# First chunk of two column tiles summed on TensorE, their loads issued sooner, and matmuls on constants ahead of and between the first column sums

## The reference

```python
mod = c @ w_mod + b_mod
shift, scale, gate = jnp.split(mod, 3, axis=-1)
u = x * (1.0 + scale[:, None, :]) + shift[:, None, :]
proj = u @ w_in
q, k, v, z_a, cb, cc, cx, z_b, g_a, g_b = jnp.split(proj, SEG_SPLITS, axis=-1)
...
h = sigmoid(g_a) * (yA @ P_a) + sigmoid(g_b) * (yB @ P_b)
out = h @ w_out
y = LayerNorm(alpha * x + gate[:, None, :] * out)
```

## Time and profile before

| | |
|---|---|
| median of 3 runs | 1502.29 us (1502.23 to 1502.61) |
| the profiled execution | 1502.2 us, of which the span of instructions is 1500.5 us |
| TensorE busy | 1477.4 us, 98% of the span |
| VectorE, ScalarE, GpSimd busy | 864.6, 511.9, 48.5 us |
| HBM read and written | 211.33 and 7.34 MB |

### The profile page before, as it was taken

The page is one execution under the profiler, slowest core; times in us unless marked ns, Lnnn a source line. Parts: engine busy times, 40 slices in busy tenths (PEclk is TensorE's granted clock), DMA queues, the critical chain, the costliest instruction groups (busy, mean ns, idle before and its releaser), DMA issues.

```text
span 1500.5 us, 18355 instructions
## 1 busy us (share of the span) xinstructions
PE 1477.4 (98%) x6592; PEld 1210.0 (81%) x6592; DVE 864.6 (58%) x1190; ACT 511.9 (34%) x724; POOL 48.5 (3%) x91
## 2 busy tenths in 40 slices
PE   6999999999999999999999999999999999999996
PEld 5888888878888788887888878888788888888885
DVE  7987877567565675656746568333432323444447
ACT  2334654253442534425344253232122221421120
POOL 0000000000000000000000000100000000000000
PEclk9999999999999999999999999999999999999999
DMA  9999543443544425444254442542223232363222
GB/s 355 392 330 318 189 117 116 137 136 90 161 120 136 137 86 154 130 133 140 84 152 134 133 141 78 188 150 91 84 88 108 92 103 85 110 252 112 84 84 112
DMA packets 211974, 219.18 MB, mean 146 GB/s; under 512 B 8417, under 2 KB 160353, under 8 KB 211169
## 3 DMA queue, kind: packets, MB, share of 16 engines
q1 hardware_dynamic: 200736, 176.72, 36.1%
q0 software_dynamic: 10096, 35.66, 7.8%
q10 hardware_dynamic: 1106, 6.32, 1.0%
HBM read 211.33 MB, written 7.34 MB: 146 GB/s over the span
## 4 chain that ended last, share of the span: by engine, by line
PE 97%; DVE 1%; SPq 1%; DMA 1%; issue 0%; ACT 0%; DVEq 0%
PE acc L1336 30%; PE acc L1338 30%; PE acc L1337 30%; PE sc L1468 1%; PE misc L1491 1%; PE sc L1336 1%; PE sc L1338 1%; PE sc L1337 1%; PE sc L1482 1%; DMA raw<-in_w_in 1%; SPq L388 0%; DVE mod_sum L840 0%; PE misc L1474 0%; PE misc L1338 0%; PE misc L1336 0%; PE misc L1337 0%
## 5 line engine op out<-in xcount | busy, mean ns | idle before, releaser
L1336 PE MATMUL acc<-act_hi,w_hi 128*128 128x512 f32 x1472 | 577.9, 393 | 2.7 <-DVE act_lo L887 2.7
L1338 PE MATMUL acc<-act_hi,w_lo 128*128 128x512 f32 x1472 | 573.8, 390 | 0.0
L1337 PE MATMUL acc<-act_lo,w_hi 128*128 128x512 f32 x1472 | 573.7, 390 | 0.0
L524 ACT ACTIVATE w_hi<-raw 128x1024 fp32r<-128x1024 f32 (+2 forms) x258 | 268.2, 1047 | 745.1 <-PE acc L1338 572.7
L813 DVE TENSOR_TENSOR w_lo<-raw,w_hi 128x1024 fp32r<-128x1024 f32 x254 | 306.5, 1215 | 370.0 <-ACT w_hi L524 369.5
L1336 PEld LDWEIGHTS acc<-act_hi,w_hi 128*128 128x128 f32 x1472 | 276.9, 188 | 64.4 <-DVE w_lo L813 4.4
L1338 PEld LDWEIGHTS acc<-act_hi,w_lo 128*128 128x128 f32 x1472 | 276.7, 188 | 58.2
L1337 PEld LDWEIGHTS acc<-act_lo,w_hi 128*128 128x128 f32 x1472 | 276.9, 188 | 56.9 <-issue 0.2
L1069 DVE SCALAR_TENSOR_TENSOR bias_acc<-bias_w,mod,bias_acc 128x512 f32<-128x512 f32 x48 | 36.0, 751 | 124.5 <-DMA bias_w<-in_w_in 124.5
L1336 PE MATMUL acc<-y_hi,w_hi 128*128 128x512 f32 x256 | 99.7, 389 | 0.0
L1338 PE MATMUL acc<-y_hi,w_lo 128*128 128x512 f32 x256 | 99.6, 389 | 0.0
(11 more groups left out here) (182 smaller groups left out, 1090.4 us busy)
## 6 DMA issues: line engine op xcount, KB each, us to landing
raw<-in_w_in SPq DMA_DIRECT2D x258, 256.0 KB, 6.3
raw<-in_w_tail SPq DMA_DIRECT2D x32, 1024.0 KB
raw<-in_w_in SPq DMA_DIRECT2D x25, 1024.0 KB
w_mod_in<-in_w_mod SPq DMA_DIRECT2D x32, 512.0 KB, 8.7
w_mod_in<-in_w_mod SPq DMA_DIRECT2D x16, 1024.0 KB, 7.7
gate_in<-in_w_mod POOLq DMA_DIRECT2D x32, 512.0 KB, 4.1
bias_w<-in_w_in POOLq DMA_DIRECT2D x48, 256.0 KB, 3.3
res<-in_x ACTq DMA_DIRECT2D x1, 4096.0 KB, 14.8
```

The lines of the kernel that those rows point to most:

```text
L524: return act.activation(dst, src, ACT.Copy)
L1336: pe.matmul(dst, a_hi, b_hi, start=first, stop=False)
L1337: pe.matmul(dst, a_hi, b_lo, start=False, stop=False)
L1338: return pe.matmul(dst, a_lo, b_hi, start=False, stop=last)
```

## The change

- **TensorE at work on constants.** VectorE sets `cos`, 512 columns wide, to 1/128 as its first instruction (before: 128 columns, later). When that is done, TensorE runs 4 float32 matmuls on it with 256 moving columns (`keep_awake(4)`), and one more after each of the first three chunks of `first_columns`. They write to `acc`, which the first products overwrite.
- **Chunk 4 (chunk 0 of group 1) summed by TensorE.** After `first_products(0, 0)`, `direct_columns` sums it for k tiles 2 and 3, by 8 float32 matmuls of moving size 1 into two columns of `misc`. VectorE leaves its four steps out, and adds the two columns to the bias just before it sums the last chunk of group 1 (`add_direct_sums`).
- **Loads.** Chunk 4 is issued between the first tiles 0 and 1; chunks 8 to 11 go ahead of x and the raw weights of group 2. The two raw pieces of tile 0 have a semaphore each.
- **VectorE's order.** `pair_columns(1)` stands ahead of `lo_half(2)`, and all four chunks of group 2 ahead of `lo_half(4)` and `lo_half(5)`.
- **TensorE's order.** For group 2 the first of the three `sc` tiles of `gate_half(1)` is done ahead of `reduce_sums(2)`, the other two behind it.

```diff
-            for n in range(MOD_CHUNKS):
+            scale_chunk(MOD_CHUNKS)
+            first_tile(1)
+            for n in range(1, MOD_CHUNKS):
                 scale_chunk(MOD_CHUNKS + n)
             x_pair(1)
             pair_unit(1)
-            for g in range(2, GROUPS):
+            for n in range(MOD_CHUNKS):
+                scale_chunk(2 * MOD_CHUNKS + n)
+            x_pair(2)
+            pair_unit(2)
+            for g in range(3, GROUPS):
...
+            dve.memset(cos[:, :], 1.0 / P).then_inc(means_set, 1)
             own(dve.memset(eps_col[:, :], EPS))
...
+            def add_direct_sums():
+
+                dve.wait_ge(b_ready, 1)
+                dve.wait_ge(direct_sums, 1)
+                own(dve.tensor_tensor(b_col[:, KT + 2:KT + 4], misc[:, 2 * KT:2 * KT + 2], b_col[:, KT + 2:KT + 4],
+                                      ALU.add))
+                settle()
...
-            for n in range(MOD_CHUNKS):
+            for n in range(DIRECT, MOD_CHUNKS):
+                if n == MOD_CHUNKS - 1:
+                    add_direct_sums()
                 scale_sums(1, n)
+            pair_columns(1)
             lo_half(2, 0, 0, 0)
-            pair_columns(1)
             scaled_lo(1)
             lo_half(3, 0, 0, 0)
-            scale_sums(2, 0)
-            scale_sums(2, 1)
-            scale_sums(2, 2)
+            for n in range(MOD_CHUNKS):
+                scale_sums(2, n)
             lo_half(4, 0, 0, 0)
             lo_half(5, 0, 0, 0)
-            scale_sums(2, 3)
...
+            def keep_awake(times):
+
+                for _ in range(times):
+                    pe.matmul(acc[:, 0, 0:2 * P], cos[:, 0:P], cos[:, 0:2 * P], start=True, stop=True)
+
+            pe.wait_ge(means_set, 1)
+            keep_awake(4)
             pe.wait_ge(ones_set, 1)
...
                     ins.then_inc(first_sums, 1)
+                    if n < MOD_CHUNKS - 1:
+                        keep_awake(1)
...
+            def direct_columns():
+
+                pe.wait_ge(mod_ready, 2)
+                for k in range(2):
+                    for n in range(DIRECT):
+                        pe.wait_ge(scale_landed[MOD_CHUNKS + n], 16)
+                        for a in range(MOD_STEPS):
+                            e = MOD_STEPS * n + a
+                            ins = pe.matmul(misc[:, 2 * KT + k:2 * KT + k + 1],
+                                            scale_in(MOD_CHUNKS + n)[:, a, k * P:(k + 1) * P], c_col[:, e:e + 1],
+                                            start=(e == 0), stop=(e == DIRECT * MOD_STEPS - 1))
+                ins.then_inc(direct_sums, 1)
+
             first_columns()
             first_products(0, 0, acc_banks)
+            direct_columns()
             first_products(0, 1, sc_banks)
             first_products(1, 0, acc_banks)
             for g in range(1, GROUPS):
+                if g == 2:
+                    gate_half(1, (0,))
                 reduce_sums(g, 2, misc[:, 2 * g:2 * g + 2])
                 if g == 1:
                     first_products(1, 1, sc_banks)
                 else:
-                    gate_half(g - 1)
+                    gate_half(g - 1, (1, 2) if g == 2 else range(G_TILES))
```

More of the change, by code:

```diff
@@ L60 @@
 SHIFTS = D // COLS
-SCALE_STEPS = GROUPS * MOD_CHUNKS * MOD_STEPS
+DIRECT = 1
+SCALE_STEPS = (GROUPS * MOD_CHUNKS - DIRECT) * MOD_STEPS
 Y_PARTS = (((0, 1024), (1024, 2048)),) * (NT - 1) + (((0, 1024), (1024, 1664), (1664, 2048)),)
@@ L231, in decoder_block @@
         first_x = sem("first_x")
-        first_raw = sem("first_raw")
+        first_raw = [sem(f"first_raw{n}") for n in range(2)]
         first_hi = sem("first_hi")
@@ L235, in decoder_block @@
         first_sums = sem("first_sums")
+        direct_sums = sem("direct_sums")
+        means_set = sem("means_set")
         b_ready = sem("b_ready")
@@ L375, in first_tile @@
                 row = w_in[k * P:(k + 1) * P, GATE_A:GATE_A + (4 + G_TILES) * P]
-                landed, each = (raw_landed[0], 32) if k else (first_raw, 16)
-                sp.dma_start(raw[:, 0, k, :], row[:, 0:COLS]).then_inc(landed, each)
-                sp.dma_start(raw[:, 0, 2 + k, 0:G_TILES * P], row[:, COLS:COLS + G_TILES * P]).then_inc(landed, each)
+                for n, (c0, c1) in enumerate(((0, COLS), (COLS, (4 + G_TILES) * P))):
+                    sp.dma_start(raw[:, 0, 2 * n + k, 0:c1 - c0], row[:, c0:c1]
+                                 ).then_inc(raw_landed[0] if k else first_raw[n], 32 if k else 16)
             def scale_chunk(c):
                 g, n = divmod(c, MOD_CHUNKS)
[L383 to L386, removed]
+                before = c - SCALE_SLOTS
+                if 0 <= before < MOD_CHUNKS:
+                    sp.wait_ge(first_sums, before + 1)
+                    sp.wait_ge(mod_step, MOD_STEPS * (before + 1))
+                elif MOD_CHUNKS <= before < MOD_CHUNKS + DIRECT:
+                    sp.wait_ge(direct_sums, 1)
+                elif before >= MOD_CHUNKS + DIRECT:
+                    sp.wait_ge(mod_step, MOD_STEPS * (before + 1 - DIRECT))
                 rows = w_mod[n * MOD_STEPS * P:(n + 1) * MOD_STEPS * P, D + g * G_COLS:D + (g + 1) * G_COLS]
@@ L582, in _ @@
                     else:
-                        act.wait_ge(first_raw, 32)
+                        act.wait_ge(first_raw[f], 16)
                     copy(w_hi[:, f, k, 0:width], raw[:, 0, 2 * f + k, 0:width]).then_inc(hi_ready if k else first_hi, 1)
@@ L826, in _, with steps_before, sum_chunk @@
             dve.wait_ge(c_in, 16)
-            def sum_chunk(q, n, rows, width, sums):
+            def steps_before(q):
+                return MOD_STEPS * (MOD_CHUNKS * q - (DIRECT if q > 1 else 0))
+            def sum_chunk(q, n, rows, width, sums, first=0):
                 for a in range(MOD_STEPS):
-                    e = MOD_STEPS * (MOD_CHUNKS * q + n) + a
+                    e = steps_before(q) + MOD_STEPS * (n - first) + a
                     dst = mod_sum[:, q % 2, a % sums, 0:width]
                     scale = c_col[:, MOD_STEPS * n + a:MOD_STEPS * n + a + 1]
-                    if n == 0 and a < sums:
+                    if n == first and a < sums:
                         if q >= 2:
@@ L850, in scale_sums @@
                 dve.wait_ge(scale_landed[c % SCALE_SLOTS], 16 * (c // SCALE_SLOTS + 1))
-                sum_chunk(g, n, scale_in(c), G_COLS, 2)
+                sum_chunk(g, n, scale_in(c), G_COLS, 2, DIRECT if g == 1 else 0)
                 if n == MOD_CHUNKS - 1:
-                    dve.wait_ge(mod_step, MOD_STEPS * MOD_CHUNKS * (g + 1))
+                    dve.wait_ge(mod_step, steps_before(g + 1))
                     both = mod_sum[:, g % 2, 0, 0:G_COLS], mod_sum[:, g % 2, 1, 0:G_COLS]
@@ L862, in shift_sums @@
                 if n == MOD_CHUNKS - 1:
-                    dve.wait_ge(mod_step, MOD_STEPS * MOD_CHUNKS * (GROUPS + j + 1))
+                    dve.wait_ge(mod_step, steps_before(GROUPS + j + 1))
                     dve.sem_inc(sums_ready, 1)
@@ L947, in bring_down @@
                 dve.tensor_scalar(table[:, :], table[:, :], -3.1415925, None, ALU.max).then_inc(trig_ready, 1)
-            own(dve.memset(cos[:, 0:P], 1.0 / P))
-            settle()
+            dve.wait_ge(means_set, 1)
             own(dve.tensor_copy(mean_mat[:, :], cos[:, 0:P]))
@@ L1361, in half, with gate_half @@
                         ins.then_inc(bank_full[n], 1)
-            def gate_half(g):
+            def gate_half(g, tiles=range(G_TILES)):
                 f = 2 * g + 1
                 pe.wait_ge(lo_ready, f + 1 + RAW_START)
-                for n in range(G_TILES):
+                for n in tiles:
                     cols = slice(n * P, (n + 1) * P)
@@ L1372, in gate_half @@
                                     act_hi[:, k, :], act_lo[:, k, :], k == 0, k == KT - 1)
-                ins.then_inc(half_done, 1)
+                if n == G_TILES - 1:
+                    ins.then_inc(half_done, 1)
             for events in (v_turned, o_done, p_turned, scores_done, half_done):
                 pe.sem_inc(events, BASE)
+            def keep_awake(times):
[3 more added lines that the diff above has]
+            keep_awake(4)
             pe.wait_ge(ones_set, 1)
```

## The result

The changed kernel is slower: 1507.44 us, median of six runs (1503.66 to 1509.24), against 1502.26 us for six runs of the kernel before (1501.13 to 1504.91). The ratio is 1.0027, 95% interval 1.0017 to 1.0037. The profiled execution, with 1503.66 us (span 1502.0) the fastest of the six, already loses 1.5 us; the typical one loses some 4 more. Later, 12 more runs on another chip gave a ratio of 1.0017 (1.0008 to 1.0025), on medians of 1505.60 and 1503.34. There the kernel before reached from 1501.4 to 1506.7 us: the three runs of the forecast (0.4 us apart) had shown too little of its spread.

The account below looks back on a forecast made before the run. TensorE, busy for 1477.4 of 1500.5 us, was taken as the bound. `half` of group 2 starts 3.2 us sooner, less 1.85 for lost clock, leaving 1.35: 1502.2 - 1.3 = 1500.9 us, range 1498.7 to 1503.9.

Parts of the forecast that it names:

- Columns: First column sums on TensorE: higher clock assumed, 0.8 us per lot of eight, first `mod` at 10.9 against 12.35 before.
- the burst: Four matmuls on constants ahead of the column sums: start at 2.6, end at 6.0, clock up by their end.
- m0: Time of `mod` of the first column: 12.35 before, 10.7 to 15.7 possible, taken as 10.9.
- the rival: Column sums in `first_columns` run slowly: half slow up to 1503.8 us, chance 0.20; wholly slow 1505.7, chance 0.10.
- turning point: Time of the first `mod` at which the change turns from gain to loss: 12.2.
- Columns wholly slow: Clock never rises in the column sums: first `mod` at 15.7, 3.5 us slower, 1505.7 us; chance 0.10.
- Up to `half` of group 1: From the first `mod` to `half` of group 1: 16.6 us, so it starts at 27.5 against 27.88.
- the relief of VectorE: Four steps of 0.40 us spared before group 1's sums: gives nothing by itself, costs TensorE 1.6 us.
- Group 2: `half` of group 2 starts at 41.2 against 44.37, 3.2 us sooner; the 3.65 us wait becomes 0.7 and 3.0.
- What is late next: Wait before `half` of group 2 loses the clock, 1.85 us; group 3 starts 1.35 sooner; later stages have room.
- No further wait of TensorE: Sign for the profile after: TensorE waits nowhere else after the 3 us for `act_lo` before `half` of group 2.
- The rule of the Trainium skill: Wait before `half` of group 2: by it 3.0 us keeps the clock, saving 3.2 us; that rival had chance 0.25.

Follow-up runs that it names:

- e0: The changed kernel again, unaltered, 12 runs on another chip against the kernel before: 1505.60 us, ratio 1.0017; its profiled execution took 1505.24 us.
- e3: The changed kernel with the four matmuls on constants ahead but without the three between: 1505.53 us, ratio 1.0009 to the kernel before.
- e1: The changed kernel without any matmuls on constants, neither the four ahead nor the three between: 1504.29 us, ratio 1.0006 to the kernel before.
- e4: Only the new orders on the kernel before, without matmuls on constants, direct sum or earlier load of chunk 4: 1501.40 us, ratio 0.9988.
- e11: The changed kernel without matmuls on constants, plus six wide matmuls before `half` of group 2 and the bias reduction in three lots: 1501.74 us, ratio 0.9992.
- e9: The kernel before with one edit, `pair_columns(1)` ahead of `lo_half(2)`: 1503.35 us against 1503.47, ratio 1.0001.
- e6: The changed kernel with two matmuls on constants after each of the first three chunks in place of one: 1507.62 us, ratio 1.0026 to the kernel before.
- e7: e4 with the 24 one-column instructions of the bias reduction dealt out in three lots of eight: 1501.01 us, ratio 0.9984 to the kernel before.
- e2: The kernel before with only the matmuls on constants added, four ahead and one after each of the first three chunks: 1504.45 us, ratio 1.0015.
- e10: e4 with 13 one-column matmuls in the wait ahead of `half` of group 2: 1500.55 us, ratio 0.9987 to the kernel before.

## Why the prediction was wrong

**Columns: the step that failed.** I put the first `mod` at 10.9. The profiles have 12.54 and 15.70. Three terms were off. The columns began at 6.28 for 6.0, since the burst started later and took 3.6 us. At the higher clock a lot of sums took 0.81 to 0.92 us and a matmul on constants 0.5, for 0.80 and 0.43, so even with the clock held all through m0 would have been 11.4. And the clock was not held: I argued that 0.8 us between single matmuls is less than the 2.0 us of idleness after which it had fallen. But those 0.8 us are filled with column sums, and at the beginning of the kernel before 7 us of them had not raised the clock, a row that I used for the rival and not against my own term. With 12.54 the turning point that I had named, m0 = 12.2, was passed even in the fastest of the six runs. The burst was as dense as the first products, but in the profile of e0 it raised nothing in the sums.

**The chance.** "Columns wholly slow" got 0.10 at 1505.7 us and lay outside the range. The chance was much too low, the price was about right: e0's profile is this case, with 1505.24 us, and five of its 12 runs show a mean granted clock of 0.996 to 0.997 as that profile does and lie at 1505.2 to 1505.8 us. The first six runs hold something more. Four lie at 1506.8 to 1509.2, with a granted clock of 0.991 to 0.994, and none of them was profiled, so what makes the median of 1507.44 stays open in part. The nearest profile is e3's (0.994): sums at the lower clock, 8.4 us for `half` of group 2 and the 1.6 us at the bias reduction, in 1506.29 us. With the three matmuls on constants that it lacks (3 x 0.86 = 2.6 us) that would be 1508.9, an estimate. The prediction counted the clock's loss once at group 2, at 1.85 us, and at no later place.

**Up to `half` of group 1: form right, sizes a little short.** The chain from m0 was forecast as 16.6 us; it took 17.5 and 16.8. `direct_columns` was forecast as 1.6 and took 1.71, `first_products(0, 0)` as 4.56 and took 5.2 in the first profile, 4.5 in e0's. That the relief of VectorE gives nothing by itself and costs TensorE its own length was right; the profiles of e1, e4 and e11 fit it. The consequence should have been drawn at this place: a sure cost of 1.6 us had nothing to set against it but an earlier m0.

**Group 2: right.** VectorE's stretch was forecast as 13.7 us and `half` of group 2 starts 13.7 us behind `half` of group 1 in every profile with the new orders; the wait of 3.65 us split into 0.3 and 2.9 (forecast 0.7 and 3.0); the clock was lost there for 1.7 us (forecast 1.85) in the first profile, kept in e4's. The loads behaved too: raw weights of group 2 at 32.0 (forecast 32.1), no wait for them.

**What is late next: missed.** I looked at the second shift sum and not at the third. In the kernel before TensorE reached it at 155.35 without a wait; in ten of the 13 profiles since it waits there for 0.3 to 1.3 us, 0.9 in e9's too, which has only one edit of the order. "No further wait of TensorE" was wrong.

**The rule of the Trainium skill** that short gaps leave the clock up (its page "TensorE: Matmul & The Clock Gate", section "Why this matters for your kernels", as in the prediction): the wait of 2.8 to 2.9 us kept the clock in e4 and lost it in the profiles after, e0, e1, e3, e6 and e7. The rule does not hold here for a gap of this length: the clock was lost in six profiles of seven.

## What to carry to other kernels

Work moved off a busy engine gains only if somebody waits for that engine at that place; look up when the result is fetched (here 26.85, ready at 24.5) before paying for the move on the engine that bounds. Matmuls on constants are free where the bounding engine would be idle anyway. In the wait ahead of `half` of group 2 the clock held in all three profiles with them, and was lost in six of seven without any; their gain in time by themselves (0.3 us) can't be told from nothing. In front of or between work that it must do, each is a sure cost for an uncertain clock. And where the clock is in play, three runs that agree are no measure of the spread: take ten of each.

## What the runs showed of the hardware

The same program gets its higher clock at different moments in different executions: after the same burst of 3.6 us from 2.71, the sums behind it ran at 0.12 us an instruction in one execution (8 in 0.92 us) and at 0.20 (8 in 1.57 us) in another. And TensorE can lose the clock while the profile shows it busy without a gap: in the first profile after the change it fell at 9.9 us, and in two of the 11 profiles with the 24 one-column instructions near 966 us in one row it fell at the end of that row (971.1 us in e3's, 969.2 in e2's), at a price of 1.6 us. Whether those instructions are the cause stays open. For it: in nine profiles 7 us of first column sums did not raise the clock, and none of the three profiles with the row dealt out has the fall. Against it: nine profiles with the row have no fall either, and the direct test (e10) did not decide it.
